# Key selection moved beside the even projection's jobs, biases and mask added by identity matmuls, output turned inside the next projection

## The reference

```python
def even_mixer(h, ...):
    aq, ak, av, iq, ik, iw, bq, bk, bv = split(h @ w_in)   # 512,512,512,512,64,8,512,512,512
    aq, ak, ik, bq, bk = rmsnorm per head of 64, with gains
    # A, 8 heads: each query keeps 64 keys
    score = sum_heads(iw * 8**-0.5 * relu(iq @ ik.T * 64**-0.5))      # per query and key
    sel = top_k(score where key chunk <= query chunk, 64)
    out_a = softmax(aq @ ak.T * 64**-0.5 + bias, over sel) @ av
    # B, 4 heads of width 128, two maps each
    lam = exp(sum(lq1*lk1)) - exp(sum(lq2*lk2)) + lambda_init
    out_b = (softmax(bq0 @ bk0.T * s + bias) - lam * softmax(bq1 @ bk1.T * s + bias)) @ bv
    out_b = rmsnorm per head of 128(out_b) * gain * (1 - lambda_init)
    return concat(out_a, out_b) @ w_out
```

## Time and profile before

| what | value |
|---|---|
| runs | 1746.64, 1747.04, 1747.14 us; median 1747.04 |
| profiled execution | 1735.48 us, span 1733.9 us |
| TensorE busy | 1653.0 us, 95% of the span |
| VectorE, ScalarE busy | 1066.8 us (62%), 853.1 us (49%) |
| share of the chain that ended last | PE 88%, DVE 5%, DMA 2%, ACT 2% |
| HBM | 171 GB/s over the span |

### The profile page before, as it was taken

How to read it: one execution, slowest core, us unless ns; L and a number is a source line. 1 busy time by engine, 2 the same in 40 slices (tenths; PEclk the granted TensorE clock), 3 DMA queues, 4 the chain that set the end, 5 groups by cost and what they waited for, 6 DMA issues and landing times.

```text
span 1733.9 us, 25053 instructions
## 1 busy us (share of the span) xinstructions
PE 1653.0 (95%) x10412; PEld 1486.4 (86%) x10412; DVE 1066.8 (62%) x1545; ACT 853.1 (49%) x1223; POOL 23.6 (1%) x26
## 2 busy tenths in 40 slices
PE   7988988999999999997989999999999999999998
PEld 7876877899989998885777999889998878789997
DVE  5555658688756564676757665455554766766553
ACT  4454645666545443553446544354443555664442
POOL 0000002000000000000000000000000000000000
PEclk9988989999999999997689999999999999999999
DMA  7747223555554555442033554545554542525553
GB/s 272 275 146 245 101 98 146 190 187 180 187 191 163 179 190 193 177 172 95 1 131 137 194 189 176 194 173 191 173 192 170 194 146 74 190 102 187 178 194 122
DMA packets 42976, 290.21 MB, mean 167 GB/s; under 512 B 5048, under 2 KB 5198, under 8 KB 9968
## 3 DMA queue, kind: packets, MB, share of 16 engines
q1 hardware_dynamic: 38272, 271.93, 43.8%
q0 software_dynamic: 4592, 16.69, 2.8%
HBM read 287.51 MB, written 8.55 MB: 171 GB/s over the span
## 4 chain that ended last, share of the span: by engine, by line
PE 88%; DVE 5%; DMA 2%; ACT 2%; issue 1%; DVEq 1%; SPq 0%; POOL 0%; ACTq 0%
PE bank L454 26%; PE bank L455 26%; PE bank L456 26%; PE bank L460 7%; DMA raw<-stream_dram 2%; PE bank L724 2%; DVE low L422 1%; PE bank L1504 1%; PE bank L606 1%; DVEq L2414 1%; ACT high L411 1%; PE bank L1702 0%; DVE u L983 0%; DVE h L1109 0%; DVE u L659 0%
## 5 line engine op out<-in xcount | busy, mean ns | idle before, releaser
L411 ACT ACTIVATE high<-raw 128x2048 fp32r<-128x2048 f32 x257 | 488.9, 1914 | 535.4 <-DMA raw<-stream_dram 525.7
L422 DVE TENSOR_TENSOR low<-raw,high 128x2048 fp32r<-128x2048 f32 x255 | 582.8, 2293 | 248.1 <-ACT high L411 246.9
L454 PE MATMUL bank<-xh,high 128*128 128x256 f32 x1880 | 535.1, 285 | 1.1 <-DVE low L422 1.1
L455 PE MATMUL bank<-xl,high 128*128 128x256 f32 x1880 | 533.5, 284 | 0.0
L456 PE MATMUL bank<-xh,low 128*128 128x256 f32 x1880 | 533.5, 284 | 0.0
L454 PEld LDWEIGHTS bank<-xh,high 128*128 128x128 f32 x1880 | 362.3, 193 | 2.1 <-issue 1.5
L455 PEld LDWEIGHTS bank<-xl,high 128*128 128x128 f32 x1880 | 362.3, 193 | 0.0
L456 PEld LDWEIGHTS bank<-xh,low 128*128 128x128 f32 x1880 | 362.2, 193 | 0.0
L454 PE MATMUL bank<-high,xh 128*128 128x512 f32 (+2 forms) x528 | 206.7, 391 | 5.6 <-DVEq L2414 3.2
L456 PE MATMUL bank<-high,xl 128*128 128x512 f32 (+2 forms) x528 | 203.6, 386 | 0.0
L455 PE MATMUL bank<-low,xh 128*128 128x512 f32 (+2 forms) x528 | 203.5, 385 | 0.0
(11 more groups left out here) (229 smaller groups left out, 1555.9 us busy)
## 6 DMA issues: line engine op xcount, KB each, us to landing
raw<-stream_dram SPq DMA_DIRECT2D x257, 1024.0 KB, 4.8
band_wide_dram<-band_rows_dram POOLq DMA_DIRECT2D x1, 3072.0 KB, 30.9
t_wide_dram<-t_rows_dram POOLq DMA_DIRECT2D x1, 2304.0 KB, 15.1
u<-mem_dram POOLq DMA_DIRECT2D x2, 1024.0 KB, 5.2
bias<-band_wide_dram POOLq DMA_DIRECT2D x1, 2048.0 KB, 15.3
rel_wide_dram<-rel_rows_dram POOLq DMA_DIRECT2D x1, 1920.0 KB, 15.7
bias<-t_wide_dram POOLq DMA_DIRECT2D x1, 1536.0 KB, 8.2
bias<-rel_wide_dram POOLq DMA_DIRECT2D x1, 1280.0 KB, 7.0
```

Of the source, the lines that this page charges most:

```text
L411: act.activation(self.high[:, n % RING, :], self.raw[:, n % RING, :], ACT.Copy).then_inc(self.high_split, 1)
L422: dve.tensor_tensor(self.low[:, n % RING, :], self.raw[:, n % RING, :], self.high[:, n % RING, :].bitcast(F32), ALU.subtract).then_inc(sel ...
L454: pe.matmul(out, lh, rh, start=start, stop=False)
L455: pe.matmul(out, lh, rl, start=False, stop=False)
```

## The change

- Job order: the index queries' columns are now job 1, then a_q, a_k, b_q, b_k, a_v, b_v. The a_q and b_q rows get 64**-0.5 in their norm's factor.
- `Select` is no stage any more. `Project` calls it: units 0 to 7 (block 1 first) in jobs 3 to 6, two a job, TensorE's part after the steps k = 2 and k = 5, in banks 6 and 7. The ring of the turned rows shrinks to banks 4 and 5. ScalarE and VectorE do their part of a unit after splitting the job's weights and before draining the job. VectorE's search: part 4 in job 4, part 5 in job 5, parts 6 and 7 in job 6, parts 0 to 3 in job 7. Lambda's work is in job 6.
- `Attention`: `fill=16`. The bias, and `taken` for A, are added in PSUM by matmuls of the identity ahead of the scores (`summed`). VectorE only takes the maximum, from PSUM; ScalarE takes the exponential from PSUM.
- `TurnedResidual` replaces `Turn` and `Residual`: A's half is turned first, then step k = 0 runs, B's half is turned ahead of k = 1.

Three stages, and three meetings, fewer.

```diff
-    main = r(0, 512) + r(512, 512) + r(1536, 512) + r(2120, 512) + r(2632, 512) + r(1024, 512) + r(3144, 512)
+    main = r(1536, 512) + r(0, 512) + r(512, 512) + r(2120, 512) + r(2632, 512) + r(1024, 512) + r(3144, 512)
@@ Turn
-        return self.core.bank[self.base + g % 4]
+        return self.core.bank[self.base + g % self.ring]
@@ Project.tensor, scalar, vector
+                if self.select:
+                    self.select.tensor(pe, s, n, j)
...
             c.split_high(act, m.slot(i0 + len(kts) - 1))
+            if self.select:
+                self.select.scalar(act, s, n)
...
             c.split_low(dve, m.slot(i0 + len(kts) - 1))
+            if self.select:
+                self.select.vector(dve, s, step, n)
@@
+class TurnedResidual(Residual):
+    def input_wait(self, pe, s, k):
+        if k == 0:
+            self.turn.turn_rows(pe, s, 0)
+        pe.wait_ge(s["turned_by_dve"], NB if k < self.kts // 2 else 2 * NB)
+        if k == 1:
+            self.turn.turn_rows(pe, s, 1)
+    def scalar(self, act, s):
+        self.turn.copy_high(act, s, 0)
+        self.turn.square_rows(act, s, 1)
+        self.core.split_high(act, self.m.first)
+        self.turn.copy_high(act, s, 1)
+        super().scalar(act, s)
+    def vector(self, dve, s):
+        self.turn.copy_low(dve, s, 0)
+        self.turn.scale_rows(dve, s, 1, Steps(dve, s["dve_step"]))
+        self.core.split_low(dve, self.m.first)
+        self.turn.copy_low(dve, s, 1)
+        super().vector(dve, s)
@@ Attention.tensor
+            for n, bias in enumerate(u.summed):
+                mm(pe, ps, c.ident, bias, n == 0, False)
             for j in range(u.n):
-                last = mm(pe, ps[:, j, :], u.q[j], u.k[j], True, True)
+                last = mm(pe, ps[:, j, :], u.q[j], u.k[j], not u.summed, not u.summed or j == u.n - 1)
@@ Attention.vector
-                step(dve.tensor_reduce(c.nmax[:, u.cols], ps, AX.X, ALU.max, negate=True))
+                largest = dve.tensor_reduce(c.nmax[:, u.cols], ps, AX.X, ALU.max, negate=True)
+                if u.scale == 1.0:
+                    largest.then_inc(s["logits_ready"], 1)
+                    return
...
-            if self.select and i < 8 and i % 2 == 0:
-                self.select.search(dve, step, 4 + i // 2)
@@
-class Select(Stage):
+class Select:
+    FIRST = 3
+    UNITS = [(b, pair) for b in (1, 0) for pair in ((0, 2), (1, 3), (4, 6), (5, 7))]
+    TILES = (2, 5)
+    PARTS = {4: (4,), 5: (5,), 6: (6, 7), 7: (0, 1, 2, 3)}
+    LAMBDA = 6
+    def tensor(self, pe, s, n, k):
+        if not self.of_job(n) or k not in self.TILES:
+            return
+        i = self.of_job(n)[self.TILES.index(k)]
+        if i == 0:
+            pe.wait_ge(s["turned_by_act"], 2)
+            pe.wait_ge(s["turned_by_dve"], 2)
+        if i >= 2:
+            pe.wait_ge(s["keys_positive"], i - 1)
+        for j, h in enumerate(pair):
+            last = mm(pe, c.bank[6 + i % 2][:, j * S:j * S + nk], self.q(h)[:, b * P:(b + 1) * P],
+                      self.k(h)[:, 0:nk], True, True)
+        last.then_inc(s["keys_scored"], 1)
+    def scalar(self, act, s, n):
+        for i in self.of_job(n):
+            act.wait_ge(s["keys_scored"], i + 1)
+            if i >= 2:
+                act.wait_ge(s["keys_summed"], i - 1)
+            act.activation(self.positive(i)[:, :, 0:nk], ps, ACT.Relu, scale=DH ** -0.5)\
+               .then_inc(s["keys_positive"], 1)
+        if n == self.LAMBDA:
+            act.wait_ge(s["lam_sums"], 1)
+            act.activation(c.small[:, 146:148], c.small[:, 144:146], ACT.Exp).then_inc(s["lam_exps"], 1)
+    def vector(self, dve, s, step, n):
+        if n == self.LAMBDA:
+            self.lam_sums(dve, s, step)
+        for i in self.of_job(n):
+            dve.wait_ge(s["keys_positive"], i + 1)
...
+        for part in self.PARTS.get(n, ()):
+            self.search(dve, step, part)
+        if n == self.LAMBDA:
+            self.lam(dve, s, step)
@@ even_mixer
-    st += [Lambda(c), select]
-                                  DH ** -0.5, P, fin, slice(at, at + 2), c.bias[:, slice(8 + pair[0], 10 + pair[0]), S - nk:S]))
+                                  1.0, P, fin, slice(at, at + 2),
+                                  summed=[c.bias[:, slice(8 + pair[0], 10 + pair[0]), S - nk:S]]))
-                              DH ** -0.5, DH, scaled(c, dst), slice(at, at + 2), c.bias[:, heads, S - nk:S],
-                              extra=c.taken[:, b, 0:nk].unsqueeze(1).to_broadcast([P, 2, nk])))
-    st.append(Attention(c, units, select))
-    st.append(out_turn(c, 8, PARAM(c.param, "subln"), norms))
+                              1.0, DH, scaled(c, dst), slice(at, at + 2), summed=[c.bias[:, heads, S - nk:S], taken]))
+    st.append(Attention(c, units, fill=16))
```

More of the change, by code:

```diff
@@ L910, in __init__ @@
         self.x, self.jobs, self.loads = x, jobs, loads
[L911 removed]
+        self.turn = Turn(core, batches or [None] * len(jobs), base=4, ring=2 if select else 4)
         ends = [j[0].ends_slot(j[1] + len(j[2]) - 1) for j in jobs]
@@ L1447, with __init__ @@
 class Unit:
-    def __init__(self, q, k, v, parts, scale, dv, finish, cols, bias=None, minus=False, extra=None):
+    def __init__(self, q, k, v, parts, scale, dv, finish, cols, bias=None, minus=False, extra=None, summed=()):
+        self.summed = summed
         self.q, self.k, self.v, self.parts, self.scale, self.dv = q, k, v, parts, scale, dv
@@ L1461, with __init__ @@
 class Attention(Stage):
-    def __init__(self, core, units, select=None, loads=None, fill=0):
+    def __init__(self, core, units, loads=None, fill=0):
         super().__init__(core)
-        self.fill = fill
-        self.units, self.select, self.loads = units, select, loads
+        self.units, self.loads, self.fill = units, loads, fill
     def gpsimd(self, pool, s):
@@ L1665, with __init__ @@
     OUT_BANK = 4
-    def __init__(self, core, units, fill, select=None, loads=None):
-        super().__init__(core, units, select, loads)
+    def __init__(self, core, units, fill, loads=None):
+        super().__init__(core, units, loads)
         self.groups = fill
@@ L2048, in __init__ @@
         self.score = c.xn[:, 1, 0:HALF].rearrange("p (b k) -> p b k", b=NB)
         self.best = c.xn[:, 1, HALF:HALF + 16].rearrange("p (b k) -> p b k", b=NB)
-        self.w = c.square[:, 2, 0:16].rearrange("p (b h) -> p b h", b=NB)
-        self.units = [(b, pair) for b in range(NB) for pair in ((0, 2), (1, 3), (4, 6), (5, 7))]
-    def tensor(self, pe, s):
-        c = self.core
-        for i, (b, pair) in enumerate(self.units):
+        self.w = c.square[:, 2, HALF:HALF + 16].rearrange("p (b h) -> p b h", b=NB)
@@ new lines, in positive, with of_job @@
+    def positive(self, i):
+        return self.core.square[:, i % 2, HALF:D].rearrange("p (j k) -> p j k", j=2)
+    def of_job(self, n):
+        first = 2 * (n - self.FIRST)
+        return [i for i in (first, first + 1) if 0 <= i < len(self.UNITS)]
+    def tensor(self, pe, s, n, k):
+        if not self.of_job(n) or k not in self.TILES:
+            return
+        c = self.core
+        i = self.of_job(n)[self.TILES.index(k)]
+        b, pair = self.UNITS[i]
+        nk = (b + 1) * P
+        if i == 0:
[7 more added lines that the diff above has]
+        last.then_inc(s["keys_scored"], 1)
@@ new lines, in scalar @@
+            ps = c.bank[6 + i % 2][:, :].rearrange("p (j k) -> p j k", j=2)[:, :, 0:nk]
+            act.activation(self.positive(i)[:, :, 0:nk], ps, ACT.Relu, scale=DH ** -0.5)\
[4 more added lines that the diff above has]
+    def vector(self, dve, s, step, n):
+        if n == self.FIRST:
+            for b in range(NB):
+                step(dve.tensor_scalar(self.w[:, b, :], self.weights(b), 8 ** -0.5, None, ALU.mult))
+        if n == self.LAMBDA:
+            self.lam_sums(dve, s, step)
+        for i in self.of_job(n):
+            b, pair = self.UNITS[i]
+            nk = (b + 1) * P
+            dve.wait_ge(s["keys_positive"], i + 1)
+            for j, h in enumerate(pair):
+                r, score, w = self.positive(i)[:, j, 0:nk], self.score[:, b, 0:nk], self.w[:, b, h:h + 1]
@@ L2205, in first_units, with head_batch @@
     return units, base
-def head_batch(c, at, width, t0, gain, head=DH):
+def head_batch(c, at, width, t0, gain, head=DH, factor=1.0):
     segments, groups = [], []
@@ L2250, in memory_stages, with even_turn, groups @@
     return out
[L2253 to L2262, removed]
+def even_turn(c):
+    def groups(q, need, gain):
+        return [(need and need + b, [c.o[:, b, (q + j) * P:(q + j + 1) * P] for j in range(4)], P, "pair",
+                 (c.oh[:, q:q + 4, block_cut(b)], c.ol[:, q:q + 4, block_cut(b)]), gain) for b in range(NB)]
+    norms = [(c.o[:, b, HALF:D].rearrange("p (h d) -> p h d", d=P), 1.0 - LAMBDA_INIT) for b in range(NB)]
+    return Turn(c, [((), groups(0, 0, None)), (norms, groups(4, 1, PARAM(c.param, "subln")))])
 def dram_row(dram, name):
```

(2 more changed lines are left out.)

82 lines of the change are left out of this document (39 added, 43 removed).

## The result

| | runs | median us | range | ratio to the kernel before, 95% interval |
|---|---|---|---|---|
| changed | 4 | 1729.71 | 1724.65 to 1731.56 | 0.9903 [0.9877, 0.993] |
| before, beside it | 4 | 1746.84 | 1742.2 to 1747.14 | |
| changed, again | 9 | 1729.97 | 1725.19 to 1732.87 | 0.9921 [0.9896, 0.9947] |
| before, beside it and the first experiments | 14 | 1744.74 | 1727.23 to 1749.12 | |
| before, beside the later experiments | 34 | 1742.63 | 1730.23 to 1748.37 | |

The change makes the kernel faster: by 17.1 us of medians in the first comparison, 14.8 against the 14 runs of before that stand beside the second group, 12.7 against the 34 later ones. The forecast was 10.7.

A forecast was written before the change was run, and what follows sets the result against it. TensorE holds nearly the whole span, at full clock but for a few slices. Selection, attention, clock and turning terms bring even_out's full rate from 877.4 to 866.7: 10.7 less, 1747.04 to 1736.3 us; range 1727 to 1747.

The forecast's parts named there:

- Jobs with selection: Projection jobs: eight score units add 6.8 us and a wait 0.6, so TensorE alone would end job 7 at 803.2.
- The wait of unit 0: Job 3: the first score unit waits 0.6 us for VectorE's half of the turned queries, copied last in its norm chain.
- VectorE's backlog: End of job 7: VectorE's queue runs to 810.8, TensorE is empty for 7.8 us, attention starts at 811.1, not 814.67.
- Identities: Even attention: identity matmuls for bias and `taken` add 15.4 us (bounds 15.4 and 18.9), giving 48.5 at full clock.
- The rule of the Trainium skill: Identity matmuls in attention: each half would add its weight load, 5.1 us over 48 halves, giving 1741; the prediction weighed against it.
- The clock at attention's start: Start of even attention: the clock is low for 5.2 us after TensorE's empty stretch, a loss of 2.6 us.
- 3 to 7 us, then 1.0 to the end: Sign to look for in even attention: granted clock 0.5 for 3 to 7 us at its start, then 1.0 to the end.
- The turning: Start of even_out: 2.9 us until k = 0, 1.2 for the second eight transposes, 0.4 for clock risk; full rate at 866.7.
- The other side of the sum: Kernel before: full rate of even_out at 877.4; median of runs 0.67% above the profiled execution, same difference taken off the forecast.
- the clock stayed low: Rival, even attention: clock stays low after the empty stretch; 36.9 us low gives 1752.1, decides from 26 us; chance 0.14.
- VectorE did not keep up: Rival, projection jobs: VectorE keeps up, attention starts 1.1 after 803.2 at full clock, giving 1726.9; chance 0.08.
- The slower side: Whole kernel: the outcome that the change makes it slower than before; chance 0.14.

The follow-up runs named there:

- the variant without the empty stretch: Changed kernel with the search of block 0 moved from job 7 into attention's first four iterations, identities kept: 1723.73 us, ratio 0.9882 to the kernel before.
- selection alone: Kernel before with only selection and lambda inside the jobs (additions on VectorE, no fill, turning a stage of its own): 1730.38 us, ratio 0.9945.
- the second trace of before: Kernel before run again with no edit: 1743.93 us, ratio 1.0025 to its 34 runs; profiled span 1743.1.

## Why the prediction was right, and where it was not

The median lay in the range and 6.6 us below the forecast. It came out near through two errors of opposite sign, which is partly luck: the changed kernel was 5.5 us slower than its sum, and the kernel before had 7.4 us in its usual execution that the trace read did not show. Counted from the end of job 2 (731.2 after, 736.8 before) to the full rate of even_out, the forecast gave the changed kernel 129.9 us; it took 135.4.

- *Jobs with selection.* TensorE alone: 66.4 forecast, 68.4 measured. The units are as priced. What was missing is the handover back: the first fast float32 matmul behind a unit takes 0.43 in the chain in place of 0.23. The lines are these, a score unit in job 3 and the matmul behind it:

```profile
737.00 1.10 PE bank L461 x4
738.10 0.43 PE bank L455
```

  Eight of them are 1.6. The wait of unit 0 for VectorE's copy was forecast at 0.6; TensorE idled 0.85.

- *VectorE's backlog.* The core of the forecast, and right to 0.6 us. VectorE ends the search and begins its last drain 73.8 after job 2; 73.2 forecast. The timeline, first round of the last four parts, the last one, the drain and attention's first maximum:

```profile
799.02 0.29 DVE L2169 MAX8 xn<-xn 128x8 f32<-128x128 f32 x1
...
804.37 0.09 DVE L2170 MATCH_VALUE_LOAD xn<-xn 128x8 f32 x1
804.44 0.27 DVE L2170 MATCH_REPLACE8 xn<-xn 128x128 f32<-128x128 f32 x1
804.75 0.23 DVE L2172 TENSOR_SCALAR taken<-xn 128x128 f32<-128x128 f32 x1
805.01 0.75 DVE L991 TENSOR_SCALAR u<-bank,inv 128x512 f32<-128x512 f32 x1
808.33 0.42 DVE L1611 TENSOR_REDUCE nmax<-bank 128x2 f32<-128x256 f32 x1 [2.57 <-PE bank L461]
```

  TensorE's empty stretch was 6.4 where 7.8 was forecast, only because TensorE's own end came 2.0 later. Attention starts 74.8 after job 2, forecast 74.3. The experiment that moved the search closed the stretch.

- *Identities.* 15.4 forecast, by columns. The bias identity of 512 columns takes 0.96 in front of a score, and bias and `taken` together 1.81 (844.84 to 846.65; first a unit without the mask, then a masked one):

```profile
818.01 1.02 PE L461 MATMUL bank<-bias,const 128*128 128x512 f32 x2
818.97 1.13 PE L461 MATMUL bank<-t 64*128 64x256 f32 x4
...
844.84 1.02 PE L461 MATMUL bank<-bias,const 128*128 128x512 f32 x2
845.70 1.02 PE L461 MATMUL bank<-taken,const 128*128 128x512 f32 x2
846.65 1.13 PE L461 MATMUL bank<-t 64*128 64x256 f32 x4
```

  With 0.53 alone and 0.96 for the two at 256 columns it is 17.0 in all at full clock, between the two ends given; attention at full clock would be 50.2 (55.3 less 5.1 of low clock), 48.5 forecast. The rule of the Trainium skill weighed there ("TensorE: Matmul & The Clock Gate", Part 3, The mechanism: weight loads that overlap only where the row groups differ, an estimated 5.1 more) is not borne out: 1.6 more were measured. That the identities only give back what the clock and VectorE had cost was said in the prediction; undoing them showed that they cost more than that, 13.6 us.

- *The clock at attention's start.* 5.2 us low were forecast, 10.9 came, 5.1 lost for 2.6. The step assumed that dense matmuls of any kind raise it within some 5 us. It rose at the end of the fill, and in the kernel without the fill only after 17.1 us of dense plain float32 matmuls. The sign "3 to 7 us, then 1.0 to the end" did not come true.

- *The turning.* 2.7 until k = 0 for 2.9 forecast; the wait for the norm was covered whole. But the clock fell as k = 0 began (3.68 us at 0.54, 1.7 lost) where 0.4 was set for it. 5.3 in all for 4.5.

- *The other side of the sum,* the step that failed most: "The median of the runs shown is 0.67% above it; I take the same difference off." The difference was not a constant. The profiled execution of before was one in which the clock rose at 851.54; in most, by their mean clock, it does not, and that is 7.4 us that the change takes away and the prediction could not see in one trace. Its chance for a low clock was spent on the changed kernel alone, when the kernel before was the one that had it.

The rivals: the clock stayed low 11 us of attention, not 26. VectorE did not keep up. The slower side was never near. Two of their figures are off in the prediction, and nothing hangs on them: attention at the low clock throughout loses 48.5 for 2.6, which gives about 1782 and not 1778, and job 6's new work on VectorE adds up to 7.2, not 8 (7.1 in the trace).

What stays open: why the clock rose at 851.54 in one execution of before and not in the other, with the same instructions; why it fell 2 us into attention in the variant without the empty stretch; and how much of the gain of selection alone is the search taken out of attention, since that was not tried apart from the scores.

## What to carry to other kernels

Work of VectorE that is moved beside TensorE's matmuls is hidden only up to the room in VectorE's own queue: write down, job by job, when that queue ends, and the overflow comes out at the next meeting. Work moved from VectorE to TensorE to spare it did not pay here, where TensorE was the bound: with block 0 searched in attention, both additions on TensorE were 13 us slower than a split of the two (mask on TensorE, bias on VectorE), and both on VectorE 3 us slower, which is not clear of the scatter. A stretch at the low clock makes every TensorE price in it wrong by two, and it can differ between executions of the same kernel: compare the mean granted clock of the timed runs with that of the profiled one before taking its sum over.

## What the runs showed of the hardware

- The same kernel had its even attention at 0.50 for 37 us in one execution and from selection to even_out in another; its timed runs lie between 1730 and 1748 and follow their mean granted clock (0.972 to 0.959).
- Scores and identities in plain float32, back to back, did not keep the clock (it fell 2 us into attention with TensorE busy throughout) and did not raise it in 6.9 us. In the second trace of before TensorE was busy 55.1 of 56.1 us of attention (817.37 to 873.50) at 0.50 throughout. The clock rose during or right behind the 16 fast float32 matmuls of 256 columns in the changed kernel, in the kernel before with the fill, and in two of the variants. Without them the changed kernel had 20.5 us at the low clock, 17.1 of them in attention.
- A fast float32 matmul right behind a plain float32 score unit takes 0.43 us in the chain in place of 0.23, at full clock.
